# The value weights of a key/value compression loaded in two parts, around the last page of values

## What is computed

```python
def compress_blocks(kv_cmp, cmp_pos_emb, w_cmp_k, w_cmp_v, k_norm_cmp_g):
    blk = pad_to_blocks(kv_cmp) + cmp_pos_emb[None, None, :, None, None, :]
    kc = jnp.einsum('bnlkd,lde->bnke', blk[:, :, :, 0], w_cmp_k)
    vc = jnp.einsum('bnlkd,lde->bnke', blk[:, :, :, 1], w_cmp_v)
    return rmsnorm(kc, k_norm_cmp_g), vc
```

## Time and profile before

| | us |
|---|---|
| median of three runs | 720.0 |
| lowest, highest | 719.45, 723.92 |
| the profiled execution, by the device's clock as the runs are | 721.7 |
| its span, from the first to the last instruction | 720.0 |
| TensorE busy in it | 679.6 (94%) |
| VectorE, ScalarE, POOL busy | 280.5, 170.3, 277.3 |
| mean granted clock of TensorE | 0.985 |

### The profile page before, as it was taken

One profiled execution on the slowest core, in us unless ns is written; L12 is line 12 of the kernel. 1 busy time (PEld: TensorE's weight loads), 2 busy tenths in 40 slices (PEclk: granted clock), 3 DMA queues, 4 the chain that ended last, 5 costly groups with the idle time before them and its releaser, 6 DMA issues.

```text
span 720.0 us, 14980 instructions
## 1 busy us (share of the span) xinstructions
PE 679.6 (94%) x5708; PEld 341.1 (47%) x5708; DVE 280.5 (39%) x746; ACT 170.3 (24%) x359; POOL 277.3 (39%) x429
## 2 busy tenths in 40 slices
PE   6999999999979889998999998999999999999993
PEld 3555455874667556877555454333333333333320
DVE  1200036038668877877121146214102500530036
ACT  3100031137647563643022120001000100010100
POOL 2456246988488674873000003403400610200060
PEclk9999999999999999999999989999999999999997
DMA  9968605047940599999892165999999999999975
GB/s 291 274 169 250 186 20 117 10 145 224 232 119 3 159 300 313 299 271 271 297 428 77 58 249 183 350 411 388 415 410 418 421 422 405 419 425 409 403 252 203
DMA packets 90206, 192.50 MB, mean 267 GB/s; under 512 B 17017, under 2 KB 60441, under 8 KB 83853
## 3 DMA queue, kind: packets, MB, share of 16 engines
q1 hardware_dynamic: 72133, 150.10, 58.7%
q0 software_dynamic: 13136, 33.30, 14.5%
q10 hardware_dynamic: 4864, 8.13, 3.0%
HBM read 174.63 MB, written 17.25 MB: 266 GB/s over the span
## 4 chain that ended last, share of the span: by engine, by line
PE 57%; DVE 6%; issue 1%; ACT 1%; DMA 1%; DVEq 0%; ACTq 0%
PE bank L1482 34%; PE bank L1376 8%; PE bank L1318 2%; DVE xh L2462 2%; PE bank L1396 1%; PE bank L1221 1%; PE bank L1520 1%; PE bank L1367 1%; PE bank L1405 1%; PE bank L1254 1%; PE bank L1224 1%; DVE arena L2206 1%; DMA proj<-normed_rows,idx 1%; PE bank L1213 1%; PE bank L1196 1%
## 5 line engine op out<-in xcount | busy, mean ns | idle before, releaser
L1482 PE MATMUL bank<-arena,proj 128*32 128x512 f32 x1728 | 238.0, 596 | 0.9 <-issue 0.8
L1482 PEld LDWEIGHTS bank<-arena,proj 128*32 128x32 f32 x1728 | 66.9, 110 | 121.1 <-issue 120.4
L996 PE MATMUL bank<-arena,amT 128*128 128x454 f32 x256 | 101.2, 553 | 0.8 <-DVE amT L1878 0.8
L2716 POOL DMA_INDIRECT proj<-normed_rows,idx_of_quads x40 | 44.8, 1120 | 140.4 <-DVE proj L2421 125.3
L2607 POOL DMA_DIRECT2D arena<-in_cache_cmp_kv x128 | 68.7, 537 | 52.0 <-issue 44.3
L996 PEld LDWEIGHTS bank<-arena,amT 128*128 128x128 f32 x256 | 48.6, 193 | 49.4 <-issue 48.1
L1482 PE MATMUL bank<-amT,proj 128*32 128x512 f32 x288 | 70.1, 592 | 0.0
L2614 POOL DMA_DIRECT2D arena<-in_cache_slc_kv x96 | 56.9, 595 | 19.0 <-issue 6.5
L2430 DVE TENSOR_TENSOR proj<-proj,bank 128x512 f32<-128x512 f32 x12 | 8.3, 688 | 137.7 <-PE bank L1482 137.7
L2627 POOL COPY arena<-arena 128x268 f32<-128x268 f32 x64 | 37.9, 650 | 25.3 <-PE bank L993 17.8
L1482 PE MATMUL bank<-queries_and_bias,proj 128*32 128x512 f32 x288 | 42.7, 593 | 0.0
(11 more groups left out here) (417 smaller groups left out, 1028.1 us busy)
## 6 DMA issues: line engine op xcount, KB each, us to landing
arena<-in_w_down SPq DMA_DIRECT2D x24, 1024.0 KB, 17.1
arena<-in_w_up SPq DMA_DIRECT2D x10, 2048.0 KB, 17.3
arena<-in_w_gate SPq DMA_DIRECT2D x16, 1024.0 KB, 14.9
arena<-in_cache_cmp_kv POOLq DMA_DIRECT2D x128, 64.0 KB, 2.5
arena<-in_cache_cmp_kv SPq DMA_DIRECT2D x128, 64.0 KB, 2.2
arena<-in_w_gate SPq DMA_DIRECT2D x4, 2048.0 KB, 21.1
amT<-in_w_gate SPq DMA_DIRECT2D x6, 1024.0 KB, 18.7
arena<-in_w_in SPq DMA_DIRECT2D x3, 1816.0 KB, 8.9
```

The source lines that it names most:

```text
L996: last = pe.matmul(ps(("in", c, i))[0:n, 0:WC], xnT[:, k, i * P:i * P + n], w_in[c % 2][:, k, :], start=k == 0, stop=k == KC - 1)
L1482: ins = pe.matmul(dst[part, :], rows[:, part], own if q < TRIO else shared, start=start, stop=stop)
L2716: po.indirect_dma_start(xg[j % 2][:, q * QD:(q + 1) * QD], None, scratch["n2"].rearrange("n (a c) -> (n a) c", a=QUADS), bass.IndirectOffs ...
```

## The change

`load_wcmp` takes the steps to load and the semaphore to count on. The key weights are loaded as before, all 64 steps at once. The value weights are loaded in two parts: steps 0 to 15 behind the pages of user 6 (0.5 MB for both halves of the partitions), steps 16 to 63 behind the pages of user 0, the last ones on SP's queue (1.5 MB). The second part counts on a semaphore of its own, for which TensorE waits at step (1, 16), in unit 14. The wait for the key products stays ahead of the pages of user 6.

```diff
+VALUE_HEAD = 16
...
+        ld_wcmp_rest = sem("rest_of_w_cmp_v_loaded")
...
-            def load_wcmp(which):
+            def load_wcmp(which, steps, signal):
                 w = a["w_cmp_k"] if which == 0 else a["w_cmp_v"]
                 for par in range(2):
-                    sp.dma_start(w_cmp[which][64 * par:64 * par + 64, :, :], w).then_inc(ld_wcmp, 16)
+                    sp.dma_start(w_cmp[which][64 * par:64 * par + 64, steps, :], w[:, steps, :]).then_inc(signal, 16)
...
-            load_wcmp(0)
+            load_wcmp(0, slice(0, HD), ld_wcmp)
...
             for par in range(2):
                 filled(sp, ("cmp", 0, par))
-            load_wcmp(1)
             load_cmp(6, 1)
+            load_wcmp(1, slice(0, VALUE_HEAD), ld_wcmp)
             page_numbers(0)
             load_cmp(0, 1)
+            load_wcmp(1, slice(VALUE_HEAD, HD), ld_wcmp_rest)
...
             def compress(r, d):

+                if (r, d) == (1, VALUE_HEAD):
+                    pe.wait_ge(ld_wcmp_rest, 32)
                 if d == 0:
                     pe.wait_ge(ld_wcmp, 32 * (r + 1))
```

## The result

The changed kernel takes 724.9 us (median of 20 runs, 722.6 to 727.5), the kernel before 720.2 on the same chip (20 runs, 716.5 to 726.2). The ratio is 1.0053, 95% interval 1.0038 to 1.0068: slower by 3.8 us (2.7 to 4.9; the two medians alone differ by 4.7). That is within 1% of no change, and above the range given. The profiled execution's span is 723.1 us against 720.0.

The account below looks back on a forecast made before the run. The prediction took TensorE's 3.7 us wait before unit 12, for late pages held by the value weights, as the bound. 3.75 idle + 1.61 slow clock - 0.3 = 5.0, so 720.0 - 5.0 = 715.0 us; range 713.3 to 720.4.

Parts of the forecast that it names:

- SP's side: On SP's queue: first 16 weight steps issued at 187.4 or earlier by pace (187.2), page numbers 3.1 us, rest at 201.1.
- the slow issue of 0.9 us: Among SP's last pages: one issue slowed by an instruction fetch at 194.4 to 195.6; without it the rest goes at 200.2.
- Step 16: Unit 14: the rest lands by 210.4 to 212.0, before TensorE asks at 214.1, so no wait is charged.
- Idle time and slow clock: Before and in unit 12: the idle 3.75 us goes, and with it the half-speed clock's 1.61 us.
- the stop shrinks from 8.27 to 3.2: POOL behind its 48th value page: only the usual 3.2 us stop for loading page numbers remains, so the last page is issued at 200.9.
- So the queue does not fill: POOL's queue at the 48th value page: only two or three pages stand behind the first quarter of the weights.
- Slower* rival: Before unit 12: a page waiting for all the rest lands at 211.0, TensorE starts at 212.7; 722.2 us, chance 0.07.
- a queue that still fills: At POOL's 48th value page: one of two ways POOL could be 1 us later than worked out, bringing the slower outcome.
- 0.2 us between two queues: End of the value pages: POOL's last page is issued 0.2 us ahead of SP's rest of the weights.
- all pages are in at 203.9: Before unit 12: POOL's last page, issued just ahead of the rest, lands in 3.0 us, before TensorE comes at 206.73.
- the good order: All pages ahead of the rest of the weights: 5.0 us gained at unit 12's end and carried through to 715.0; chance 0.50.
- term of 0.3 for waiting on chunk copies: Unit 12: 0.3 us taken off the gain because TensorE catches up with VectorE's chunk copies.

Follow-up runs that it names:

- e3: Changed kernel, with SP waiting until all of POOL's pages have landed before it issues the rest of the value weights; ratio 0.9969 to the kernel before.
- e10: Changed kernel, with SP loading user 0's page numbers ahead of the first 16 weight steps and issuing the rest after all value pages landed; ratio 0.9968.
- e1: Changed kernel, with POOL's load of user 1's page numbers moved up behind user 3's pages; ratio 1.0064 to the kernel before.
- e9: Changed kernel, with SP loading user 0's page numbers ahead of the first 16 value weight steps, not behind them; ratio 1.0026 to the kernel before.
- a0: The changed kernel run again, unedited, on another chip; ratio 1.0056 to the kernel before.
- e11: As e9, with SP waiting only until POOL has issued, not landed, its last value page before issuing the rest of the weights; ratio 0.9951.
- e2: Changed kernel, with the rest of the value weights sent as three pairs of 16 steps instead of one pair of 48; ratio 1.0022.
- e6: A changed kernel with 6912 instead of 8192 bytes of DMA scratch memory; the text does not say which of three such variants (1.0089, 1.0085, 1.0017).
- e8: Kernel before, with 6912 bytes of DMA scratch memory and user 1's page numbers loaded behind POOL's 32nd value page; ratio 1.0027.

## Why the prediction was wrong

**What held.** SP's side: the first 16 steps went out at 187.4 (187.2 forecast), the rest at 200.9 (201.1). That is partly luck: the slow issue of 0.9 us did not come, and the page numbers took 3.4 instead of 3.1. The fetch of instructions on which the slow issue had been put (queue q8, 194.5 us in the kernel before) came at 190.8, while SP was loading page numbers and issuing nothing. The other one recurred: at 174.4 us there is such a fetch, and SP's issue at 174.8 took 1.34 us. The start of unit 12 follows the last page by 1.65 plus 0.1. Step 16 finds the rest there, with over 10 us to spare since TensorE itself was late, and with a wait of 0.2 in e3 and e10, where the rest was issued 4 to 5 us later. Idle time and slow clock do go together when the last page is early (e3, e10). That a page behind the weights lands with them held: 212.77 beside 212.40, and within 0.8 us in e1, e9 and a0.

**The step that failed** is POOL's: "the stop shrinks from 8.27 to 3.2. The last 16 run from 191.9 to 201.5 and the last one is issued at 200.9." It shrank to 5.53 and the last page went out at 203.4. Two things were missed.
- The price of the stop was taken from a load of page numbers at another place. This one has a second part, the turn of POOL's memory, and the lowest it came to was 4.4 to 4.6 us (e9, e10, e11). By that alone the last page is issued at 188.9 + 4.4 + 9.0 = 202.3, 1.4 us behind the rest; a0, with 1.6, lost as much as the changed kernel.
- "So the queue does not fill" was the wrong picture. It is not that so many pages in flight fill it; at its turn the engine waits for every page to land. Two pages behind the first 16 steps (3.9 and 5.1 us) were enough to bring 4.5 to 5.5.

The trace of before had it: the stop of 3.37 us at 70.7, where no page numbers are loaded, and its distance of 56 transfers to the 48th value page. The prediction read the earlier trace rows as a queue that backs up and did not look for a second stop without a load.

From there the *Slower* rival ran much as worked out: "a page that waits for all of the rest lands with it". It put the landing at 211.0, TensorE at 212.7 and the time at 722.2, and named "a queue that still fills" as what would bring it. Measured: 212.8, 214.5, 723.1 by the span, and 3.8 us over before by the ratio. The landing is 1.8 us later than worked out: the rest went out 0.7 later (200.9 for 200.2), took 0.7 longer to land (11.5 for 10.8), and the page landed 0.4 behind it. Its chance of 0.07 was far too small: it hung on 0.2 us between two queues, of which POOL's was worked out from a sum with a term of 3.2 us that no row of that place showed. The range ended at 720.4, below that rival.

**A second step was weaker than it looked.** That all pages are in at 203.9 when the last goes out just ahead of the rest was taken from one page that landed in 3.0 us. In e11 the last page went out 0.03 us ahead of the rest and took 5.4, and the end of unit 12 came 1.1 us earlier than before (213.09 for 214.14), not 5.0. No run of the changed order has the 0.2 us of the forecast.

**The gain that was forecast for the good order** was 5.0 us. In e10 it was 4.3 at the end of unit 12 (the term of 0.3 for waiting on chunk copies was 1.0: 209.82 - 206.73 - 2.06), 3.4 at the last value product, and 2.3 (0.4 to 4.2) at the end by the ratio of the runs.

**How the two queues share the DMA engines.** Pages behind SP's weights took up to 9.5 us again (9.9 in a0), so for the last page the outcome was that of the rows. The picture of e2 is not against taking turns, though: with the rest in six transfers, pages and transfers landed in alternation (weights at 205.0, 207.3, 208.7, 210.0, 211.3, 212.7; pages at 206.0 to 212.0), and in e11 a page was slowed by transfers issued with it. The Trainium skill, "DMA: Bandwidth & Descriptors", section "Queues, rings and completion order", has each DMA engine take turns between queues packet by packet. These runs would agree with turns of a much larger piece than the prediction had in mind. That is argued from the order of landings and not shown; how large a turn is, no run here settles.

## What to carry to other kernels

When two queues race for the DMA engines, a transfer that must be early has to be put first by a wait, not by a sum: here the order cost or gained 7 us at unit 12, and a wait of SP for POOL's pages turned a loss of 0.5% into a gain of 0.3%. Before pricing a stop by a like one elsewhere, list all stops of that engine and count the transfers between them; one that comes at a fixed count has a cause of its own. And time gained in the middle of a kernel is not the gain at the end: unit 12 began 3.8 us earlier in e10 and 1.0 in e11, and the ratios say 2.3 and 3.5 us with intervals that overlap. In the traces the stretches of slow clock behind it moved.

## What the runs showed of the hardware

- GpSimd's transfers stop at a fixed count: 56 of these 64 KB pages with 8192 bytes of `dynamic_dma_scratch_size`, 47 with 6912. Where the last landing is what it waits for, the stop ends 0.96 us (0.85 with 6912 bytes, e6 and e8) after it, and it is in no case here under 2.5 us. A load of page numbers alone takes 2.9 to 3.7 us in most cases (up to 4.3 with no weights under way, 5.6 in e8 behind weights); the two at one place take 4.4 us at least, and then end 1.95 us after the register move if all pages have landed by then.
- Pages issued 0.3 us or more behind the first of two weight transfers of 0.75 MB each on another queue take 7.6 to 9.9 us to land (changed, e9, a0) instead of 2.3 to 3.0; one issued at the same moment takes 5.4. Runs of 4 KB in place of 12 bring the last page down to 8.0.
- SP's issue of a page takes 0.8 to 1.4 us instead of 0.33 within 0.6 us after the start of a fetch of instructions on queue q8 at 172 to 176 us. This is so in all 14 traces; why is not shown.
- The DMA engines were busy for 99% of 207 to 210.8 us and moved 216 GB/s in the changed kernel, with the weights and the last pages in flight; in 422 to 429 us of the kernel before they moved 407 at 98%. At the first rate 1.5 MB take some 7 us (an estimate). Columns as above:

```profile
207.00:210.80 3.80, 0.00 (x0) 0.00 (x0) 0.00 (x0) 0.00 (x0) 0.00 (x0) 1.00 0.99 216
```
